# Sample attention with queries and probabilities on zeroed diagonals as stationary side, four heads in column tiles, and the samples' output product in column tiles

## What is computed

```python
# dilated_attn_step, for each of the 3 groups (window, dilation = 128,1; 512,4; 2048,16)
kk = concat([k_buf, k_new], axis=1); vv = concat([v_buf, v_new], axis=1)   # rows (N, Wb + T, H, Dh)
sc = einsum('nthd,ntmhd->nthm', q, kk[:, idx]) * (dh ** -0.5)              # 8 samples, 4 tokens, 4 heads, Dh = 64
sc = where(valid, sc, NEG_INF)
m = max(sc); p = exp(sc - m); den = sum(p)
o = einsum('nthm,ntmhd->nthd', p, vv[:, idx]) / den
# over the three groups: softmax of m + log(den) as weights, sum of the weighted o
# token_mixer, at the end, for prompt and samples
return merged @ p['w_out'][l]
```

## Time and profile before

| | us |
|---|---|
| median of 3 runs | 1618.36 |
| lowest, highest | 1614.91, 1623.09 |
| profiled execution, device time | 1615.49 |
| its span in the trace | 1613.7 |
| TensorE busy | 1462.1 |
| VectorE busy | 493.1 |
| sample attention, first scores to last gate unit | 570.6 to 744.6 |
| output product and routing | 1058.3 to about 1180 |

### The profile page before, as it was taken

How to read it: one execution, slowest core, us unless ns; L and a number is a source line. 1 busy time by engine, 2 the same in 40 slices (tenths; PEclk the granted TensorE clock), 3 DMA queues, 4 the chain that set the end, 5 groups by cost and what they waited for, 6 DMA issues and landing times. The chain is left out here.

```text
span 1613.7 us, 20364 instructions
## 1 busy us (share of the span) xinstructions
PE 1462.1 (91%) x8509; PEld 970.0 (60%) x8509; DVE 493.1 (31%) x1073; ACT 288.3 (18%) x670; POOL 111.8 (7%) x113
## 2 busy tenths in 40 slices
PE   5999999999999899998999989999994999999930
PEld 3556658899887567765656666668883343333310
DVE  4300001104333122366046224433454331111108
ACT  4100000003334110011231222211121111111103
POOL 0000000000120032001000000000001000000023
PEclk9799999999997898898999999999995999999965
DMA  9333224304340341132141028421007799999838
GB/s 311 111 116 119 79 81 134 100 17 146 150 168 32 95 153 56 61 111 74 33 79 49 10 90 267 144 103 54 29 27 274 269 392 381 414 416 414 353 119 243
DMA packets 131421, 253.18 MB, mean 157 GB/s; under 512 B 22505, under 2 KB 96889, under 8 KB 123122
## 3 DMA queue, kind: packets, MB, share of 16 engines
q1 hardware_dynamic: 106082, 189.67, 33.4%
q0 software_dynamic: 10560, 33.50, 6.3%
q10 hardware_dynamic: 14688, 28.71, 4.7%
HBM read 204.96 MB, written 49.63 MB: 158 GB/s over the span
## 5 line engine op out<-in xcount | busy, mean ns | idle before, releaser
L352 PE MATMUL psum<-h_t,ring 128*128 128x352 f32 x576 | 174.1, 464 | 2.7 <-DVE h_t L503 2.7
L991 PE MATMUL psum<-h_t,ring 128*128 128x352 f32 x480 | 158.6, 490 | 5.4 <-PEq L624 3.0
L352 PEld LDWEIGHTS psum<-h_t,ring 128*128 128x128 f32 x576 | 110.0, 192 | 65.5 <-issue 6.3
L2077 PE MATMUL psum<-ring,big 128*128 128x256 f32 (+1 forms) x576 | 131.2, 387 | 2.1 <-PEq L1734 2.1
L991 PEld LDWEIGHTS psum<-h_t,ring 128*128 128x128 f32 x480 | 95.9, 203 | 59.5 <-issue 13.2
L2077 PEld LDWEIGHTS psum<-ring,big 128*128 128x128 f32 (+1 forms) x576 | 105.3, 185 | 23.1 <-issue 3.2
L2164 PE MATMUL psum<-w_gate_up,u_rows 128*32 128x512 f32 x608 | 101.7, 608 | 3.3 <-DMA w_gate_up<-in_w_exp_up 1.4
L368 PE MATMUL psum<-ring,h_t 128*128 128x256 f32 (+1 forms) x432 | 103.1, 395 | 0.0
L2164 PE MATMUL psum<-ring,u_rows 128*32 128x512 f32 x576 | 101.7, 599 | 0.9 <-ACT u_rows L2285 0.9
L368 PEld LDWEIGHTS psum<-ring,h_t 128*128 128x128 f32 (+1 forms) x432 | 90.5, 266 | 8.7 <-issue 1.2
L2186 PE MATMUL psum<-big 128*32 128x512 f32 x736 | 83.7, 595 | 0.8 <-DVE big L2586 0.8
(11 more groups left out here) (464 smaller groups left out, 1879.7 us busy)
## 6 DMA issues: line engine op xcount, KB each, us to landing
big<-in_w_exp_down SPq DMA_DIRECT2D x32, 1024.0 KB, 10.8
ring<-in_w_ada SPq DMA_DIRECT2D x24, 1024.0 KB, 7.3
w_gate_up<-in_w_exp_gate SPq DMA_DIRECT2D x13, 1024.0 KB
w_gate_up<-in_w_exp_up SPq DMA_DIRECT2D x13, 1024.0 KB
ring<-in_w_exp_gate SPq DMA_DIRECT2D x13, 1024.0 KB, 8.4
ring<-in_w_exp_up SPq DMA_DIRECT2D x13, 1024.0 KB, 10.4
tmp_expert_rows<-zero_rows POOLq DMA_DIRECT2D x12, 1024.0 KB, 4.5
ring<-in_w_in SPq DMA_DIRECT2D x11, 1024.0 KB, 8.6
```

The lines of the kernel that those rows point to most:

```text
L352: m = nc.tensor.matmul(bank[(e + j) % NB][:, 0:CW], w[:, k, c * P:(c + 1) * P], ht3[:, k, j * CW:(j + 1) * CW], start=(k == 0), stop=(k == ...
L991: m = T_.matmul(bank[4 + u % 4][:, 0:CW], w_[:, k, c0:c0 + P], ht3[:, k, j * CW:(j + 1) * CW], start=(k == 0), stop=(k == KT - 1))
L2077: m = T_.matmul(bank[2 * (i % 2) + b // 2][0:r, (b % 2) * WB:(b % 2 + 1) * WB], merged_t[:, k, t * P:t * P + r], w[:, k, :], start=(k == 0 ...
```

## The change

Scores: the queries become the stationary side. `q_z` holds, for each head pair, 32 columns per sample, all zero but for the sample's own four, on a diagonal; the queries are copied there for each group. So the 32 rows of a head fill up in PSUM by accumulation over the eight samples, each of which adds its scores in its own four rows and zero elsewhere. The four heads stand in four column tiles (and two row halves), with keys moving, and the scores come out with tokens on the partitions: no transpose. Values: the turned probabilities are copied to zeroed diagonals (`pt_z`), the values move, and the accumulation over samples, blocks and new tokens gives the rows directly, without transpose and without the addition. GpSimd clears the diagonals once. Of the five gate units of a group one stands before the scores (now ahead of the wait for the copy of the turned keys), two before the turned probabilities, one before the values, one after them. VectorE's pieces move: `powers`, `b_bar`, `b_table_im` between maximum and turned probabilities, `b_table_re` after their copy in group 1, and the first four doublings of `e_re`, `e_im` after their copy in group 2. Output product: the samples' four weight blocks stand in four column tiles, in one bank; the steps of the tile after it are put in another order.

```diff
-            FILL.update({f"scores{g}": 1, f"turn_scores{g}": 1, f"turn_probs{g}": 1, f"values{g}": 1, f"rows{g}": 1, f"next{g}": 0})
+            FILL.update({f"scores{g}": 1, f"turn_probs{g}": 2, f"values{g}": 1, f"next{g}": 1})
...
+            q_z = sb("q_diagonal", [P, 2, 288], stack=st)
+            pt_z = (big[:, 0:1056], sb("pt_diagonal", [P, 1056], stack=st)[:, :])
...
+                    G.memset(q_z[:, :, :], 0.0)
+                    G.memset(pt_z[0], 0.0)
+                    G.memset(pt_z[1], 0.0).then_inc(s_zero, 1)
...
+                        fill(f"scores{g}")
                         pe.wait_ge(s_kte, kt_before[g + 1])
-                        if g:
-                            pe.wait_ge(s_or, g)
-                        fill(f"scores{g}")
+                        pe.wait_ge(s_qp, g + 1)
...
+                        for nn in range(DEC_B):
+                            for h in range(HEADS):
+                                hp, lo = h // 2, 64 * (h % 2)
+                                T_.matmul(bank[2][h * NS:(h + 1) * NS, 0:DK[g]], q_z[lo:lo + 64, hp, nn * NS:(nn + 1) * NS],
+                                          kv[lo:lo + 64, nn, hp, :], start=(nn == 0), stop=(nn == DEC_B - 1))
+                        for h in range(HEADS):
+                            hp, lo = h // 2, 64 * (h % 2)
+                            m = T_.matmul(bank[2][h * NS:(h + 1) * NS, DK[g]:DK[g] + NS], q_new[lo:lo + 64, 2 * g + hp, :],
+                                          k_new[lo:lo + 64, 2 * g + hp, :], start=True, stop=True)
+                        m.then_inc(s_sp, 1)
                         fill(f"turn_probs{g}")
...
+                        for nn in range(DEC_B):
+                            for b in range(KB[g]):
+                                for h in range(HEADS):
+                                    T_.matmul(bank[3][h * NS:(h + 1) * NS, 0:HD], pt_z[b][0:w, nn * P + h * NS:nn * P + (h + 1) * NS],
+                                              vcv[g][:, nn, b, h * HD:(h + 1) * HD], start=(nn == 0 and b == 0), stop=False)
...
-                        fill(f"rows{g}")
-                        pe.wait_ge(s_os, g + 1)
-                        nc.tensor.transpose(bank[3][:, 256:256 + HD], o2[:, :], ident[0:HD, 0:HD]).then_inc(s_orp, 1)
                         fill(f"next{g}")
...
+                        (powers, b_bar, b_table_im)[g]()
                         dve.wait_ge(s_ptp, g + 1)
...
+                        if g == 1:
+                            b_table_re()
+                        if g == 2:
+                            e_table(9)
+                        dve.wait_ge(s_op, g + 1)
+                        V.tensor_copy(d_sb[:, 0:HD], bank[3][:, 0:HD]).then_inc(s_or, 1)
...
+                def out_samples(i):
+
+                    for k in range(KT):
+                        for b in range(4):
+                            w = ring[:, b, :].rearrange("p (k c) -> p k c", k=KT)
+                            m = T_.matmul(bank[2 * (i % 2)][32 * b:32 * b + 32, 0:WB], merged_t[:, k, SEQ:N], w[:, k, :],
+                                          start=(k == 0), stop=(k == KT - 1))
+                    m.then_inc(s_op5, 1)
...
+                    if i == 1:
+                        out_samples(i)
+                        continue
+                    out_block(i, 0)
+                    if i == 2:
+                        turn_h2(0)
+                    out_block(i, 1)
+                    if i == 2:
+                        route(0)
+                        out_block(i, 2)
+                    if i >= 2:
+                        turn_h2(i - 1)
...
+                    if t == TT:
+                        for b in range(4):
+                            m = V.tensor_copy(h2[:, b * WB:(b + 1) * WB], bank[2 * (i % 2)][32 * b:32 * b + 32, 0:WB])
+                        c.step(dve, m)
+                        c.step(dve, V.tensor_tensor(h2, h2, rows_["gate1"][0:r, :], ALU.mult))
```

More of the change, by code:

```diff
@@ L1030, in _ @@
[L1030 to L1037, removed]
@@ new lines, in _, with e_table @@
+                    turn_of_slots = []
+                    def e_table(stop):
+                        if e_width[0] == 1:
+                            for _ in range(3):
+                                double()
+                            dve.wait_ge(s_ca, 1)
+                            c.step(dve, V.memset(e_re[:, :, 0], 1.0))
+                            c.step(dve, V.memset(e_im[:, :, 0], 0.0))
+                        while e_width[0] < min(stop, NCH):
+                            w_ = e_width[0]
+                            sh = [P, SP2, w_]
+                            t_ = (tmp_e if w_ > 32 else tmp_s)[:, :, 0:w_]
+                            cmul(e_re[:, :, w_:2 * w_], e_im[:, :, w_:2 * w_], e_re[:, :, 0:w_], e_im[:, :, 0:w_],
+                                 turn_of[0][0].unsqueeze(2).to_broadcast(sh), turn_of[0][1].unsqueeze(2).to_broadcast(sh), t_)
+                            e_width[0] = 2 * w_
+                            if 2 * w_ < NCH:
+                                double()
@@ L1207, in _ @@
                         V.tensor_reduce(d_sb[:, HD:HD + 1], s2[:, 0:wd], AX.X, ALU.max, negate=True).then_inc(s_nx, 1)
+                        (powers, b_bar, b_table_im)[g]()
                         dve.wait_ge(s_ptp, g + 1)
-                        V.tensor_copy(pt2[0:w, 0:KB[g], :], bank[1][0:w, 0:KB[g] * P].rearrange("p (b c) -> p b c", c=P))
-                        V.tensor_copy(pt2[0:NS, 2, :], bank[1][0:NS, 256:384]).then_inc(s_pte, 1)
-                        for piece in ((powers,), (b_bar, b_table_re), (b_table_im,))[g]:
-                            piece()
@@ L1213, in _ @@
-                        dve.wait_ge(s_oa, g + 1)
-                        V.tensor_tensor(o2[:, :], o2[:, :], bank[3][0:HD, 0:P], ALU.add).then_inc(s_os, 1)
-                        dve.wait_ge(s_orp, g + 1)
-                        V.tensor_copy(d_sb[:, 0:HD], bank[3][:, 256:256 + HD]).then_inc(s_or, 1)
-                    V.memset(merge[1][:, TT - 5].rearrange("p g h d -> p (g h d)"), 1.0).then_inc(s_clr, 1)
-                    k = 0
-                    src = (co, si)
-                    for _ in range(3):
-                        dst = (sm[:, k, :], sm[:, 14 + k, :])
-                        tt(dst[0], src[0], src[0], ALU.mult)
-                        tt(tp[:, 0:16], src[1], src[1], ALU.mult)
-                        tt(dst[0], dst[0], tp[:, 0:16], ALU.subtract)
-                        c.step(dve, V.scalar_tensor_tensor(out=dst[1], in0=src[0], scalar=2.0, in1=src[1], op0=ALU.mult, op1=ALU.mult))
-                        src, k = dst, 1 - k
@@ L1228, in _ @@
[L1228 to L1243 removed]
+                        for b in range(KB[g]):
+                            V.tensor_copy(pt_diag[b][0:w], bank[1][0:w, b * P:(b + 1) * P].rearrange("p (h n t) -> p n h t", n=DEC_B, t=DEC_T))
@@ L1313, in _ @@
                         finish(f"values{g}")
-                        act.wait_ge(s_op, g + 1)
-                        A.activation(o2[:, :], bank[2][0:HD, 0:P], ACT.Copy).then_inc(s_oa, 1)
-                        finish(f"rows{g}")
                         finish(f"next{g}")
```

120 lines of the change are left out of this document (50 added, 70 removed).

## The result

The changed kernel takes 1557.26 us as a median of four runs (1549.84 to 1558.14), the kernel before 1616.63 beside it: ratio 0.9613, 95% interval 0.9578 to 0.9649, 59 us saved. The forecast was 1560.4. The two ratios lie within each other's intervals, so the saving is known to some 5 us either way and no better. The profiled execution took 1549.84 us (span 1548.1), 65.6 less than that of before.

A forecast was written before the change was run, and what follows sets the result against it. TensorE, busy 91% of the span, was taken as the bound. Gains of 40.5 + 1.8 + 2.4 + 3.3 + 10.6 = 58.6, less 0.6, gave 58 us: 1618.4 to 1560.4 us as a median, range 1553 to 1580.

The forecast's parts named there:

- Part 1: Sample attention's scores and values in three groups: four column tiles cut 52.5 us to 12.0, gaining 40.5 us.
- the short row of 64 columns: Profile row before the change: four rounds of 64 rows x 64 columns in 0.41 us, bounding a round at 0.10.
- The upper bound (40 us): Scores and values of the samples: 40 us in all if no column tiles overlap.
- drain at a change of tiling mode: TensorE drains when tiling mode changes; no row isolates it, the 0.2 us counted per stretch would include it.
- Parts 2 and 3: Transposes of scores and rows go, 1.8 us; a gate unit ahead of the turned keys' wait saves 2.4 us.
- Part 4: VectorE's pieces move, 12.29 us of table pulled ahead in group 2; the 3.27 us wait at the merge's end goes.
- Part 5: Output product: the samples' tile falls from 14.2 to 3.5 us; gain 10.6 us, with the experts' weights moving along.
- the rivals: Half clock 0.15 (1573 or 1587 us), poor overlap 0.09 (1576 or 1564), merge chain 0.05 (1565), slower 0.03 (1642).
- The slower one: Rival for the new products: tiles don't overlap and the array counts as idle, 1642 us; chance 0.03.
- 94.7 us: The slower rival's cost of products, 2 x 40 = 80 us, plus 14.4 in the units behind, against 52.5.
- 48 less 44.3: Merge: ready 44.3 us after the last values, against 48 us of TensorE units; 3.5 us to spare was claimed.

The follow-up runs named there:

- tile_by_tile: The changed kernel with the same instructions reordered, all products of one column tile before those of the next: 1582.52 us, ratio 0.9785.
- wait_first: The changed kernel with the scores' gate unit put back behind the wait for the copied keys: 1556.67 us, ratio 0.9606.
- the second: A second measurement of the unedited changed kernel and the kernel before, six executions: 1552.07 against 1615.79 us, ratio 0.9594.

## Why the prediction was right

**Part 1, the products.** 12.0 us forecast, 11.4 measured, and every stretch within 0.2 us of its term (2, 3.7, 1.1; 1.1, 2, 1.1). The proportion from 512 columns down to 64 held: 0.055 us a round, where the short row of 64 columns had bounded it at 0.10. The upper bound (40 us) would have come nearer if the loops had stood the other way round: 34 us in tile_by_tile. Units behind the products took 4.8 to 5.0 us at clock 1.00. The gain is 52.5 - 11.4 = 41.1, forecast 40.5. That sum took the window with the clock's losses in it; counted as work alone the old products would have been 32.8, and the forecast some 20 us too slow. The Trainium skill (TensorE: Matmul & The Clock Gate, Measured speedup vs the span model) gives 2.38 times for three column tiles; at that gain for each tile the stretches and the output product would have been 4 us longer, by estimate. The trace doesn't bear it out for four: 3.66 us for 64 instructions that alone would be 64 x 0.216 = 13.8 are 3.8 times. The Trainium skill's drain at a change of tiling mode (TensorEngine Tiling (Array Packing), Key Properties) isn't isolated by any run; if it is there, it fits into what is left beside the rounds, as it was counted: 11.4 less 1.7, 3.5, 0.9 and 3.6 is 1.7 us for six new-token parts and six ends.

**Parts 2 and 3.** No transpose and no idle stands in the timeline where they were. 1.8 and 2.4 were forecast; wait_first shows the 2.4 in three idles.

**Part 4, right result, reason half wrong.** The merge's exponential was ready 30.0 us after the last values (29.5 forecast), the merge took 14.7 more (14.75), and 2.7 us are to spare (3.5). The step that failed is "In group 2 12.29 us of the table of powers are pulled ahead" as what ends the wait: without it the wait is gone as well. What ended it is the tenth unit behind the rows (47.4 us of work beside VectorE's 45.9, for 42.9 before). With the table pulled ahead, what bounds the merge is the place of ScalarE's exponential behind the fifth unit, which the prediction had in its sum but didn't name as the bound.

**From keys to merge** the parts come to 40.5 + 1.8 + 2.4 + 3.3 = 48.0; measured 49.4.

**Part 5.** 10.6 forecast, 10.7 measured in the product: the samples' tile 3.6 us, the first wait 0.93 (about 1.1), the samples' tile ready 1.3 us before TensorE came (1.4). Mis-sized is what comes behind: 13.7 us up to the experts, for the prediction took everything behind the product as moved along unchanged and didn't look at the clock there, 0.81 in its ranking and lowered again behind the search. These 3 us are luck, not an effect that was foreseen.

**The rest.** 58 us forecast, 59 by the first medians, 64 by the second. The profiled pair says 65.6, of which 3.4 are the scatter ahead of the change and 3 stand behind the output product. So that 58 and 59 agree to a microsecond is luck; the mechanism is confirmed by the stretches, each within 0.2 us. None of the rivals came. The slower one would have needed products over 70.6 us. Two sums are slightly off and change nothing: its 94.7 us are 80 + 14.4 = 94.4, and 48 less 44.3 is 3.7 to spare, not 3.5.

## What to carry to other kernels

Take the cost of a product from a window that reaches over the dense work behind it, for a thin product is paid there too; here 20 of 52 us were clock. To get them back, change the form so that many columns move for each load. To get short stretches as well, let the loop go round the column tiles innermost: the clock held in either order, but the time was three times as long in the other. Mixing dense steps into thin ones held the clock in four places and lost it in two, and cost more than it gave. And when a wait ends, ask by an experiment which of the moves ended it: here a move of 12 us of work wasn't needed.

## What was not expected of the hardware

- Up to three instructions of the next column tile start beside the last of the tile before, even if each tile's instructions stand in a row (11.5 us for 13.8).
- The same thin instructions at the same place held clock 1.00 over 4.1 us in one profile and lost it within that stretch in another (1.95 and 3.11 us for the same 16).
- Once down, the clock stayed at 0.51 over 17.3 us of thin and dense work mixed, while the same mixture with the scores held 1.00 over 12.5 us.
- Stretches of 256 and 512 instructions on TensorE with 64 or 128 columns moving had pauses of 1.1 to 1.5 us for which the profile shows no cause; 256 instructions with 256 columns had none, nor had the originals, a quarter as long.
